# Where a side stream's loads stand in an in-order load queue: pairs at their place in the even input, none behind a pooling group

## The reference

```python
def second_block(...):
    for layer in range(DEPTH_2):
        shift, scale, gate = jnp.split((s_lat @ ada_w[layer] + ada_b[layer])[:, None, :], 3, axis=-1)
        h = rms_norm(x, pre_g[layer]) * (1.0 + scale) + shift
        ...
        y = pool_conv_mixer(h, ev_w_in[e], ev_pool_w[e], ev_pool_scale[e], ev_conv_w[e],
                            ev_conv_b[e], ev_w_out[e], True)

def pool_conv_mixer(h, w_in, pool_w, pool_scale, conv_w, conv_b, w_out, on_grid):
    a_v, a_g, b_x, b_b, b_c, b_g = jnp.split(h @ w_in, idx, axis=-1)
    a_out = multiscale_pool(a_v, pool_w, pool_scale, on_grid) * jax.nn.silu(a_g)
    b_out = b_b * depthwise_conv3(b_c * b_x, conv_w, conv_b) * jax.nn.silu(b_g)
    return jnp.concatenate([a_out, b_out], axis=-1) @ w_out
```

## Time and profile before

| | |
|---|---|
| median of 3 runs | 3416.58 us (3414.7 to 3424.42) |
| profiled execution, its own time | 3416.83 us |
| its span, from first to last instruction | 3414.8 us |
| granted TensorE clock, mean | 0.986 of full speed |
| busy in the span | PE 3292.6 us, DVE 1538.0 us, ACT 1418.2 us |
| moved by DMA | 556.97 MB, mean 163 GB/s |

### The profile page before, as it was taken

How to read it: one execution, slowest core, us unless ns; L and a number is a source line. 1 busy time by engine, 2 the same in 40 slices (tenths; PEclk the granted TensorE clock), 3 DMA queues, 4 the chain that set the end, 5 groups by cost and what they waited for, 6 DMA issues and landing times.

```text
span 3414.8 us, 48335 instructions
## 1 busy us (share of the span) xinstructions
PE 3292.6 (96%) x20802; PEld 2858.3 (84%) x20802; DVE 1538.0 (45%) x1951; ACT 1418.2 (42%) x1962; POOL 31.9 (1%) x30
## 2 busy tenths in 40 slices
PE   7999999999999999999999999999799999999998
PEld 7989998699999987767787868688689888888886
DVE  5444445555555554455222222242544455453554
ACT  5444544544444444356322212132554444444443
POOL 0000002000000000000000000000000000000000
PEclk9999999999999999999999999999899999999999
DMA  6665455766666676755454544433423233232343
GB/s 208 184 191 175 150 153 169 241 213 224 228 224 230 212 262 230 244 193 189 155 172 160 170 153 146 143 141 102 135 81 102 91 100 110 90 108 91 102 135 118
DMA packets 349061, 556.97 MB, mean 163 GB/s; under 512 B 16881, under 2 KB 148977, under 8 KB 347697
## 3 DMA queue, kind: packets, MB, share of 16 engines
q1 hardware_dynamic: 346304, 540.08, 49.2%
q0 software_dynamic: 2256, 13.11, 1.0%
q10 hardware_dynamic: 288, 0.70, 0.1%
HBM read 551.60 MB, written 2.23 MB: 162 GB/s over the span
## 4 chain that ended last, share of the span: by engine, by line
PE 85%; ACT 6%; DVE 5%; issue 3%; DMA 2%; POOL 0%; SPq 0%; ACTq 0%; DVEq 0%
PE ps L688 77%; PE ps L713 3%; ACT whi L1062 2%; DVE wlo L1583 1%; PE ps L881 1%; DMA raw<-in_ada_w 1%; PE ps L744 1%; PE ps L903 1%; ACT hA L1237 1%; PE ps L885 1%; DVE hA L1819 1%; PE ps L899 1%; ACT L1237 1%; DVE hA L1811 1%; DVE hB L1808 0%
## 5 line engine op out<-in xcount | busy, mean ns | idle before, releaser
L1583 DVE TENSOR_TENSOR wlo<-raw,whi 128x1024 fp32r<-128x1024 f32 x819 | 998.6, 1226 | 1485.3 <-ACT whi L1062 1483.4
L1062 ACT ACTIVATE whi<-raw 128x1024 fp32r<-128x1024 f32 x824 | 862.3, 1057 | 1382.8 <-PE ps L688 1109.8
L688 PE MATMUL ps<-HCh,whi 128*128 128x512 f32 (+1 forms) x1664 | 607.9, 365 | 4.2 <-ACT T L1456 3.3
L688 PE MATMUL ps<-HCl,whi 128*128 128x512 f32 (+1 forms) x1664 | 596.8, 359 | 0.0
L688 PE MATMUL ps<-HCh,wlo 128*128 128x512 f32 (+1 forms) x1664 | 596.4, 358 | 0.0
L688 PE MATMUL ps<-Vh,whi 128*128 128x256 f32 x1408 | 402.2, 286 | 0.0
L688 PE MATMUL ps<-Vh,wlo 128*128 128x256 f32 x1408 | 398.3, 283 | 0.0
L688 PE MATMUL ps<-Vl,whi 128*128 128x256 f32 x1408 | 398.3, 283 | 0.0
L688 PEld LDWEIGHTS ps<-HCh,whi 128*128 128x128 f32 x1664 | 317.2, 191 | 75.4 <-issue 31.7
L688 PE MATMUL ps<-whi,HCh 128*128 128x256 f32 (+1 forms) x1152 | 376.1, 326 | 1.5 <-DVE HCl L1681 1.5
L688 PE MATMUL ps<-wlo,HCh 128*128 128x256 f32 (+1 forms) x1152 | 367.5, 319 | 0.0
(11 more groups left out here) (301 smaller groups left out, 4086.9 us busy)
## 6 DMA issues: line engine op xcount, KB each, us to landing
raw<-in_ada_w SPq DMA_DIRECT2D x192, 512.0 KB, 4.7
raw<-in_w_up SPq DMA_DIRECT2D x176, 512.0 KB, 4.6
raw<-in_w_in SPq DMA_DIRECT2D x160, 512.0 KB, 3.7
raw<-in_od_w_in SPq DMA_DIRECT2D x160, 512.0 KB, 3.5
raw<-in_ev_w_in SPq DMA_DIRECT2D x96, 512.0 KB, 5.7
raw<-in_w_down SPq DMA_DIRECT2D x88, 512.0 KB, 4.6
raw<-in_w_out SPq DMA_DIRECT2D x32, 512.0 KB, 4.6
raw<-in_w_ple_gate SPq DMA_DIRECT2D x32, 512.0 KB, 4.1
```

Of the source, the lines that this page charges most:

```text
L688: mm = e.matmul(o, a, b, start=first and t == 0, stop=last, skip_group_check=True)
L1062: e.activation(m.whi[ch.i % SPLIT][:, 0:n], m.raw[ch.slot][:, 0:n], ACT.Copy).then_inc(S("hi"), 1)
L1583: e.tensor_tensor(m.wlo[ch.i % SPLIT][:, 0:n], m.raw[ch.slot][:, 0:n], m.whi[ch.i % SPLIT][:, 0:n].bitcast(F32), ALU.subtract).then_inc(S( ...
```

## The change

The lag of a pair's loads becomes an argument of `spread`: it stays 2 for `out`, `up` and `down`, and is 0 for the even input, where a pair's two chunks are put into the load order right behind the main chunk that the pair follows on TensorE. `pw` is quiet at its only chunk, so that no pair follows it and the rate isn't counted up there. `behind` becomes a number, and for an unsplit chunk of the main stream (`ple`, `pw`) it is one more than the chunk's own: a split whose load needs such a chunk's slot is placed no earlier than at the next chunk's turn.

```diff
-ADA_LAG, LATER = 3, 2
+ADA_LAG = 3
...
-        ch.behind = behind or ch
+        ch.behind = ch.c + 1 if behind is None else behind
...
-            ch.place = -1 if ch.i < 2 else max(at, old.behind.c if old and old.i is None else 0)
+            ch.place = -1 if ch.i < 2 else max(at, old.behind if old and old.i is None else 0)
...
                 G.fill = self.ada(fill)
                 for u in G.fill:
                     for x in u.chunks:
-                        self.stream(x, behind=G.chunks[0])
+                        self.stream(x, behind=G.chunks[0].c)
...
             for u in G.after[-1]:
                 self.count(*u.chunks)
                 for x in u.chunks:
-                    x.behind = ch
-                self.held.append((self.mains + LATER, u))
+                    x.behind = ch.c
+                if self.lag:
+                    self.held.append((self.mains + self.lag, u))
+                else:
+                    for x in u.chunks:
+                        self.stream(x, behind=ch.c)
...
-    def spread(self, upto, chunks):
-
-        self.limit = upto
+    def spread(self, upto, chunks, lag):
+
+        self.limit, self.lag = upto, lag
         self.rate, self.due = (upto - self.units) / chunks, 0.5
...
-    p.spread(48, 320)
+    p.spread(48, 320, 2)
...
-    p.spread(48, 281)
+    p.spread(48, 281, 2)
...
-    p.spread(92, 92)
+    p.spread(92, 92, 0)
...
-            p.spread(92, 85)
+            p.spread(92, 85, 0)
         p.group(f"bx{j}", W, 2048 + 256 * j, 256, NT, 2 * T)
-        p.group(f"pw{j}", A["ev_pool_w"][j], 0, 256, 2, 2 * T, raw=True)
+        p.group(f"pw{j}", A["ev_pool_w"][j], 0, 256, 2, 2 * T, raw=True, quiet=(0,))
```

## The result

The changed kernel takes 3407.04 us (median of 7, 3401.95 to 3413.59) against 3418.98 us of the kernel before (7 runs). The ratio is 0.9962, 95% interval 0.9947 to 0.9977: 13 us, or 8 to 18, less. 3403.5 was forecast (range 3397 to 3413), with 13.1 us less than before.

What follows compares the result with a forecast made beforehand. TensorE, busy for 96% of the span, was taken as the bound. Removed waits (-24.3, -2.4), new waits (+12.1) and clock (+1.5) gave -13.1 us against 3416.83: 3403.5 us, range 3397 to 3413.

Steps and rivals of the forecast that it cites:

- What was lost before: Even input: 9.9 us lost at j=2, 10.3 at j=3, with waits of 2.26 and 1.79 in sum 24.3 us.
- The pairs' waits and E's go: Four waits on pairs behind the pooling groups go, -24.3 us; in the ple groups the wait for E goes, -2.4.
- The new waits: Even input: TensorE waits for ScalarE's copies behind splits: AV 2.7 us twice, T 2.8, PL 3.9; sum +12.1.
- The clock: Even input: only the 3.9 us wait for PL at j=2 costs clock; 1.5 us taken, bounds 0 and 2.8.
- Rival A: Even input: new waits at upper bounds, each dropping the clock at 2.8 us: 3415, halfway 3409; chance 0.18.
- The sum: Whole kernel: -24.3 - 2.4 + 12.1 + 1.5 = -13.1 us against 3416.83 us gives 3403.5 us.
- Rival C: Even input's rhythm: loads over 3.8 us later make TensorE wait at each of 41 pairs, 3427 and up; chance 0.05.
- B: Even input: the copies aren't late, as ScalarE reaches them earlier; only -26.7, 3390 us; chance 0.08.
- D: Even input: waits behind pw stay, as loads there are needed too soon; part of 24.3 won, 3415; chance 0.06.

Runs made afterwards that it cites:

- the copies first: The changed kernel, but ScalarE copies AV, PL and T1 ahead of the split standing before them; loads and products not moved: 3393.58 us, ratio 0.9921 to before.
- the lag of 0 everywhere: The changed kernel with AV, PL and T1 copied ahead of splits, plus lag 0 for output, up and down projections: 3416.8 us, ratio 0.999 to before.
- AV's copy first: The changed kernel, but ScalarE copies AV ahead of the split at av.3, with PL and T1 left where they are: 3397.94 us in one run.

## Why the prediction was right, and where it was off

- **What was lost before: right.** 24.3 us were read from the chain, the ruler says 24.4.
- **The pairs' waits and E's go: right,** all five, and E's gain of 2.4 is kept at ctx's load: from the first ple product to the late fill pair the changed kernel takes 2.6 us less, with the fill's own wait 0.55 longer.
- **The new waits: right in place, cause and number.** Four, for the copies at av1, bx1, bx2 and av3, none at j=0. Forecast against measured: AV 2.7 and 3.0, T 2.8 and 2.25, PL 3.9 and 3.35, AV 2.7 and 2.2, in sum 12.1 and 10.8. The first load's split started 3.68 us behind the pair (1826.27 to 1829.95) where I took 4.3, and the third's 6.78 (1975.44 to 1982.22) where I took 7.3. Both are within 0.1 us of the rows that I had at the lower end of the bounds. That ScalarE's order causes them was shown by the copies first, where all four went.
- **The clock: the term that was mis-sized.** I took 1.5 us, for one fall behind the wait of 3.9, because a wait of 2.36 had left the clock at 1.00. The profiled execution lost up to 7.3 in three falls, behind waits of 3.01, 3.35 and 2.17 us, but none behind 2.25. A length of wait that decides it can't be read from rows like mine. Rival A, more clock falls, came true in part.
- **The sum.** By this one execution the even input won 6.3 us (24.4 - 18.1) where 10.7 were forecast, and E 2.4: 8.7 together. The ratio says 13.0 (8 to 18). The gap is no contradiction, as this execution was 6.5 us over its own median and that of the kernel before 2.2 under its own. The two spans differ by 3.2 us (3414.8 and 3411.6), and the pieces add up to that within 0.1: -6.3 in the even input, -2.6 from the first ple product to the late fill pair, +2.2 of clock behind that pair, +3.4 of clock in the up projection. But no trace shows the 13.0 piece by piece. In the one execution that can be read, the even input gave 4.4 us less than forecast, for 1.3 less of waits and some 5.8 more of clock. That the total hit 13.1 so well is partly luck.
- **Rival C,** the rhythm breaking, didn't occur: no wait for wlo in the even input, in the changed kernel or with the copies first. B and D are out by the waits above.

What I had not asked was which part of the change wins. The answer turns it around. By the ruler the quiet pw takes away 20.7 of the 24.4 us; the split's later place at ple takes away the wait of 2.4 there. The lag of 0 brings all four new waits. On top of quiet pw and ple it costs about 14 us unless ScalarE's copies are put first. Then it is ahead by only the 2 us behind bc2.0 in the rulers (578.5 and 580.3), and the ratios (0.9921 and 0.9922) don't tell the two apart.

## What to carry to other kernels

When a load waits for a slot that a side product holds, ask first what else stands behind it in the order of the engine that unpacks it: in the even input all of the harm of early loads was in copies that stood behind a split that waited for its data, and none in the data. Put an engine's work that is ready ahead of work that waits for a transfer, and look for such places at the ends of groups too: the same lag of 0 cost some 23 us in the projections ahead, where nothing was moved. And try the parts of a change one by one even if it wins: one line of this one was worth more than all of it.

## What was unexpected about the hardware

Short waits of TensorE can cost clock, and their length alone doesn't say which do. The granted clock fell from 1.00 to 0.5 behind waits of 2.17 us (2119.60), of 2.31 (T, with AV's copy first), of 2.09 (with pw quiet alone, whose window 1977 to 1982 us shows 0.66) and even behind one of the ten for wlo, 1.77 us at 1181.39 with the lag of 0 everywhere (1181.4 to 1187 us: 0.70). It stayed at 1.00 behind others of 2.25, 2.26 and 2.36. Behind all twelve waits of 3.01 us and more inside the rulers of these kernels it fell. A single wait then cost up to 3.0 us more than itself in the changed kernel: the pooling products at 1801.03 took 6.64 us instead of 3.65. I had priced four waits of 12.1 us with 1.5 us of clock. Over the nine rulers, waits of 73.5 us in sum came with a rest of 35.8 us, so half of a wait's own length again would have been the better estimate; that is fitted to these same runs and no run tests it.
